# The last two pieces of every output product, multiplied by token tile instead of by piece

## The reference

```
x = layer_norm(ALPHA*x + 0.5*swiglu(x))          # 1024 -> 2816 -> 1024
y = concat(pool, gated conv, neighbourhood attention) @ w_out
x = layer_norm(ALPHA*x + y)
x = layer_norm(ALPHA*x + 0.5*swiglu(x))
```

```
x = x + 0.5*rms(swiglu(rms(x)))
x = x + rms(mixer(rms(x)))                       # MLA, GLA and RWKV branches, merged, @ w_out
x = x + rms(memory_attention(rms(x)))            # ... @ mem_wo
x = x + 0.5*rms(swiglu(rms(x)))
```

## Time and profile before

| | |
|---|---|
| median of three runs | 2997.88 us (2996.47 to 3000.35) |
| the profiled execution | 2998.23 us |
| its span, first to last instruction | 2996.4 us |
| TensorE, matmuls | 2800.4 us busy, 93% |
| VectorE | 1592.4 us, 53% |
| ScalarE | 1293.3 us, 43% |
| GpSimd | 477.8 us, 16% |
| mean granted TensorE clock | 0.965 |

### The profile page before, as it was taken

How to read it: one execution, slowest core, us unless ns; L and a number is a source line. 1 busy time by engine, 2 the same in 40 slices (tenths; PEclk the granted TensorE clock), 3 DMA queues, 4 the chain that set the end, 5 groups by cost and what they waited for, 6 DMA issues and landing times.

```text
span 2996.4 us, 51984 instructions
## 1 busy us (share of the span) xinstructions
PE 2800.4 (93%) x21700; PEld 2593.2 (87%) x21700; DVE 1592.4 (53%) x2184; ACT 1293.3 (43%) x1832; POOL 477.8 (16%) x199
## 2 busy tenths in 40 slices
PE   7999999999999999988889899999998878989998
PEld 7988899898889989987779788999988778888898
DVE  5566555656655565543545515555564274552555
ACT  3435443443543443444523454444444452344433
POOL 0000000000000000034423660000004451474000
PEclk9999999999999999998999999999999899999999
DMA  8755466675536646632322544665663331244563
GB/s 233 209 157 161 120 183 188 170 210 156 160 114 188 183 143 187 197 99 87 104 65 72 165 152 133 184 187 160 186 187 95 92 113 51 103 149 123 162 188 126
DMA packets 622827, 445.08 MB, mean 149 GB/s; under 512 B 27904, under 2 KB 589344, under 8 KB 622176
## 3 DMA queue, kind: packets, MB, share of 16 engines
q1 hardware_dynamic: 622688, 443.09, 49.8%
HBM read 441.99 MB, written 1.05 MB: 148 GB/s over the span
## 4 chain that ended last, share of the span: by engine, by line
PE 86%; DVE 9%; ACT 3%; issue 1%; DMA 0%; POOL 0%; SPq 0%; ACTq 0%; DVEq 0%; POOLq 0%
PE ps L373 19%; PE ps L374 18%; PE ps L375 18%; PE ps L389 7%; PE ps L390 7%; PE ps L391 7%; PE ps L630 1%; PE ps L606 1%; PE ps L1353 1%; ACT w_hi L645 1%; PE ps L1160 1%; PE ps L1061 1%; PE ps L1343 1%; DVE zT L1495 1%; DVE moments L908 1%
## 5 line engine op out<-in xcount | busy, mean ns | idle before, releaser
L373 PE MATMUL ps<-in_hi,w_hi 128*128 128x256 f32 x4352 | 1263.2, 290 | 69.5 <-POOL w_lo L814 31.1
L645 ACT ACTIVATE w_hi<-raw 128x1024 fp32r<-128x1024 f32 x800 | 844.9, 1057 | 947.1 <-PE ps L375 626.4
L374 PE MATMUL ps<-in_lo,w_hi 128*128 128x256 f32 x4352 | 1248.4, 287 | 0.0
L375 PE MATMUL ps<-in_hi,w_lo 128*128 128x256 f32 x4352 | 1247.6, 287 | 0.0
L814 DVE TENSOR_TENSOR w_lo<-raw,w_hi 128x1024 fp32r<-128x1024 f32 x606 | 742.7, 1226 | 742.8 <-ACT w_hi L645 741.7
L373 PEld LDWEIGHTS ps<-in_hi,w_hi 128*128 128x128 f32 x4352 | 852.9, 196 | 89.8 <-issue 32.4
L374 PEld LDWEIGHTS ps<-in_lo,w_hi 128*128 128x128 f32 x4352 | 852.9, 196 | 7.3 <-issue 0.5
L375 PEld LDWEIGHTS ps<-in_hi,w_lo 128*128 128x128 f32 x4352 | 851.9, 196 | 0.0
L814 POOL TENSOR_TENSOR w_lo<-raw,w_hi 128x1024 fp32r<-128x1024 f32 x194 | 477.2, 2468 | 2270.5 <-ACT w_hi L645 2269.7
L389 PE MATMUL ps<-w_hi,hid_hi 128*128 128x512 f32 x704 | 276.0, 392 | 0.0
L390 PE MATMUL ps<-w_lo,hid_hi 128*128 128x512 f32 x704 | 275.9, 392 | 0.0
(11 more groups left out here) (302 smaller groups left out, 2665.8 us busy)
## 6 DMA issues: line engine op xcount, KB each, us to landing
raw<-in_w_ffn_in SPq DMA_DIRECT2D x176, 512.0 KB, 3.8
raw<-in_w_mix SPq DMA_DIRECT2D x112, 512.0 KB, 3.8
raw<-in_ffn_w_gate SPq DMA_DIRECT2D x88, 512.0 KB, 4.1
raw<-in_ffn_w_up SPq DMA_DIRECT2D x88, 512.0 KB, 3.8
raw<-in_ffn_w_down SPq DMA_DIRECT2D x88, 512.0 KB, 3.6
raw<-in_w_ffn_out SPq DMA_DIRECT2D x88, 512.0 KB, 3.4
raw<-in_w_in SPq DMA_DIRECT2D x40, 512.0 KB, 3.8
raw<-in_w_out SPq DMA_DIRECT2D x32, 512.0 KB, 3.5
```

The lines of the kernel that those rows point to most:

```text
L373: nc.tensor.matmul(o, lh, rh, start=first, stop=False, **kw)
L374: nc.tensor.matmul(o, lh, rl, start=False, stop=False, **kw)
L375: return nc.tensor.matmul(o, ll, rh, start=False, stop=last, **kw)
L645: nc.scalar.activation(w_hi[:, e % SPLIT, :], raw[:, e % RAW, :], ACT.Copy).then_inc(sem("split_high"), 1)
```

## The change

The last two pieces of each output product are no longer multiplied one after the other. Both are multiplied into banks 0 and 1 (first 128 tokens) and then both into banks 2 and 3. The new function `last_two` writes the order out, and both `pe_rows` and `pe_ffn` end with it; for this the last round of the hardware loop in `pe_ffn` is taken out of the loop. `piece_used` of A is counted after A's matmuls on bank 3, in the second half, and that of B at the very end, as before. The wait for B's split and, in a SwiGLU, for the last hidden tile stands ahead of B's matmuls on bank 0.

```diff
--- before.py
+++ after.py
@@ -392,16 +392,33 @@
 
         def pe_rows(pe, e0, chunk):
 
-            for k in range(KD):
+            for k in range(KD - 2):
                 e = e0 + k
                 pe.wait_ge(sem("split_low"), e + 1)
                 pe.wait_ge(sem("in_ready"), chunk + k // 2 + 1)
                 for b in range(4):
-                    mm = three_rows(b, e, in_hi[:, k, :], in_lo[:, k, :], k == 0, k == KD - 1)
-                    if k == KD - 1 and b < 3:
-
-                        mm.then_inc(sem("rows_out"), 1)
+                    mm = three_rows(b, e, in_hi[:, k, :], in_lo[:, k, :], k == 0, False)
                 mm.then_inc(sem("piece_used"), 1)
+            pe.wait_ge(sem("in_ready"), chunk + KD // 2)
+
+            def ready(i):
+                pe.wait_ge(sem("split_low"), e0 + KD - 1 + i)
+
+            last_two(e0 + KD - 2, ready, [(in_hi[:, k, :], in_lo[:, k, :]) for k in (KD - 2, KD - 1)])
+
+        def last_two(e, ready, left):
+
+            for t in range(HALF):
+                for i in range(2):
+                    if t == 0:
+                        ready(i)
+                    for b in (2 * t, 2 * t + 1):
+                        mm = three_rows(b, e + i, *left[i], False, i == 1)
+                        if i == 1 and b < 3:
+
+                            mm.then_inc(sem("rows_out"), 1)
+                    if t == HALF - 1:
+                        mm.then_inc(sem("piece_used"), 1)
 
         WARM_BANK = 5
 
@@ -465,26 +482,31 @@
                                    k == 0, k == KD - 1)
                     mm.then_inc(sem("piece_used"), 1)
 
-            def down(j, it=0, last=False):
-                e = e0 + (FFN_PIECES - 1 if last else 3 * j + 4)
+            def hidden(j, e, it=0):
                 pe.wait_ge(sem("split_low"), e + 1 + it * RAW)
 
                 pe.wait_ge(sem("hidden_ready"), (ffn0 + n) * TILES + j + 1 + it * 2)
+
+            def down(j, it=0):
+                e = e0 + 3 * j + 4
+                hidden(j, e, it)
                 for b in range(4):
-                    mm = three_rows(b, e, hid_hi[:, j % 2, :], hid_lo[:, j % 2, :], j == 0, last)
-                    if last and b < 3:
-
-                        mm.then_inc(sem("rows_out"), 1)
+                    mm = three_rows(b, e, hid_hi[:, j % 2, :], hid_lo[:, j % 2, :], j == 0, False)
                 mm.then_inc(sem("piece_used"), 1)
 
             begin()
             gate_up(1)
             down(0)
-            with pe.Fori(0, TILES // 2 - 1) as it:
+            with pe.Fori(0, TILES // 2 - 2) as it:
                 for j in (2, 3):
                     gate_up(j, it)
                     down(j - 1, it)
-            down(TILES - 1, last=True)
+            gate_up(TILES - 2)
+            down(TILES - 3)
+            gate_up(TILES - 1)
+            e = e0 + FFN_PIECES - 2
+            last_two(e, lambda i: hidden(TILES - 2 + i, e + i), [(hid_hi[:, j % 2, :], hid_lo[:, j % 2, :])
+                                                                 for j in (TILES - 2, TILES - 1)])
 
         def pe_linear(pe, q0, e0, groups, chunk, together=1):
```

## The result

The changed kernel takes 3011.58 us (median of six runs, 3010.26 to 3012.01); the kernel before, run beside it, 2998.97 us (2996.47 to 3000.35). The ratio is 1.0042 with a 95% interval of 1.0029 to 1.0055: slower by 12.6 us. A second measurement of both gave 1.0030 (1.0019 to 1.0041), some 9 us. The forecast was 3022, and the range 3010 to 3031: the time lies in it, 10.4 us under the forecast and 1.6 us above the lower end.

What follows compares the result with a forecast made beforehand. TensorE is busy 93%; its tails end by a chain: A released, copy, subtraction, four banks. 13.6 + 4.8 - 1.3 + 2.4 + 4.5 = +24.0 us on 2998.23 gave 3022, range 3010 to 3031.

Steps and rivals of the forecast that it cites:

- Release of A, ten tails at 1.36: Six layer-norm and four second-block tails: A released two groups later delays copy, subtraction, norm and transposes; 13.6 us.
- The tail between the layers costs only the stall: Second block, between layers: fillers run up to the transposes, so A's later release costs nothing there.
- The stall, 8 x 0.6: Eight SwiGLU tails: TensorE waits for the last hidden tile before B's first group; 4.8 us.
- The last tail, -1.3 + 0.6: Kernel's end: banks 0 and 1 finished earlier gain 1.3 us; the stall of 0.6 is counted separately.
- B's split in time in the projections: Six products without a stall: B's split is ready when its group wants it; costed at nothing.
- The branch products, +2.4: Two branch-output products: GpSimd's moved subtraction delays the next chunk and the tail by 1.2 us each.
- The clock, +4.5: Longer TensorE idle before the transposes brings three half-clock falls more, 4.5 us; between none and 9 us.
- a fall costs 1.5 us: Price of one half-clock fall, from first transpose to first hidden matmul: 17.06 against 15.56 us.
- Faster: Rival: the norm starts on the early banks under TensorE's last groups; about -24 us, 2974; 4%.
- No change: Rival: A's later release is absorbed, leaving stalls and the last tail's gain; +3.5 us, 3001; 5%.
- Half of it: Rival: the 1.36 us holds, but the stall is under 0.3 and branch products gain; +12, 3010; 11%.
- The clock dominates: Rival: every exposed tail loses one more low stretch, 15 us in place of 4.5; +34.5, 3032; 12%.

Runs made afterwards that it cites:

- release_five: Changed kernel with group order A0 A1 A2 B0 A3 B1 B2 B3, A released after five groups; 1.0002 of the kernel before, +0.6 us.
- pure_delay: Kernel before, TensorE untouched; in ten tails VectorE subtracts or ScalarE copies twice for the piece replacing A; 1.0013 of before, +3.9 us.
- rows_only: Kernel before with the new order only in the six output projections (`pe_rows`); 1.0018 of before, +5.4 us.
- no_stall: Changed kernel with order A0 A1 A2 B0 B1 A3 B2 B3, three groups of A before B's first; 1.0023 of before, +6.9 us.
- ffn_only: Kernel before with the new order only in the eight SwiGLU products (`pe_ffn`); 1.0031 of before, +9.3 us.
- more_fillers: Changed kernel with five fillers more after each product, not between layers of the second block; 1.0040 of before.
- norm_first: Changed kernel, norm ahead of the split for A's successor on ScalarE and VectorE, GpSimd subtracting in the first block, fewer fillers; 2970.28 us, 0.9896 of before.
- norm_first_no_stall: norm_first with group order A0 A1 A2 B0 B1 A3 B2 B3; 2971.78 us beside 2966.83 for norm_first on the same chip.
- norm_first_old_order: Kernel before, its order A then B kept, with norm_first's rearrangement of ScalarE, VectorE, GpSimd and fillers; 2981.74 us, 0.9935 of before.

## Why the forecast was right, and where it was not

**Release of A, ten tails at 1.36: right.** The projections show it pure: +1.36 in each of four; release_five has half of it, and pure_delay lengthens the chain by 1.26 or 1.09 without a change on TensorE, and the tails with it. **The tail between the layers costs only the stall: right**, +0.69, and rows_only and no_stall have 14.97 and 15.01 there. **The stall, 8 x 0.6: right** to a tenth: the tail lengthens by 0.62 to 0.68, of which 0.58 is the gap on TensorE. The tails that have both show 2.05 to 2.07 where 1.96 was forecast. **The last tail, -1.3 + 0.6: right**, -0.62. These terms sum to 17.1 in the forecast and 17.9 in the traces.

**B's split in time in the projections: right.** TensorE's groups by line for the changed kernel (busy us, mean ns of one, idle before and what ended it): the first matmul of a group, first in the SwiGLUs, then in the projections:

```profile
L389 PE MATMUL ps<-w_hi,hid_hi 128*128 128x512 f32 x704 | 276.8, 393 | 3.4 <-DVE hid_lo L896 3.4
...
L389 PE MATMUL ps<-w_hi,in_hi 128*128 128x512 f32 x192 | 75.3, 392 | 8.8 <-DVE in_lo L868 7.8 <-ACT arena L811 0.9
```

The first idles 8 x 0.42 = 3.4 us, all for hid_lo; the second never for a piece's w_lo.

**The branch products, +2.4: the size and the sign were wrong.** The first in_lo is short and the next chunk's products end late, as told, but the second chunk is 0.75 late, not 1.2: in_lo gained 1.35, the two products lost 2.97 - 0.87 = 2.10. And between the branch product's A and the memory product's A the time is 0.6 shorter: 0.75 later by the chunk, and 3.4 us less at the lower clock, which at 0.41 each are 1.4 (an estimate from the rows above, not shown by a run). So -0.6 and -0.5 instead of twice +1.2. The forecast put a delay of a chunk down as a delay of the stage; what the stage lasts also depends on where in it the clock falls. The Trainium skill, "SBUF — State Buffer", section "SBUF: two separate sides", says that of VectorE and GpSimd whoever starts first blocks the other for a whole instruction. These rows agree with it within 0.3 us. An in_lo of 0.68 alone came when a GpSimd subtraction of 2.4 us, begun at 1708.74, had some 0.6 us to go, and took 1.06, where the rule would give some 1.25 (an estimate, 0.57 + 0.68); two products of 0.87 alone took 2.97 with one subtraction beside them, where it would give some 3.3 (2.40 + 0.87).

**The clock, +4.5: wrong in sign, and the main miss.** The forecast took three falls more, each at 1.5 us, the difference of the two rows of one tail. By count it was near: the changed kernel has 218 and 225 us at half clock in its two traces, the kernel before 210 and 208. The price was wrong. The traces have the same stretch, from the first transpose after the memory product to the first hidden-tile matmul, in both layers of every kernel:

| kernel | idle before the transposes | clock falls on | stretch |
|---|---|---|---|
| before (two traces), ffn_only | 1.05 | gate matmuls (5 of 6) | 17.05 |
| | 1.05 | nothing (1 of 6) | 15.56 |
| more_fillers | 0.25 | nothing (2 of 2) | 15.56 |
| release_five | 1.72 | nothing (2 of 2) | 15.56 |
| pure_delay | 2.14 | nothing (2 of 2) | 15.55 |
| norm_first (two traces), norm_first_no_stall | 0.81, 1.42 | nothing (6 of 6) | 15.55 |
| norm_first_old_order | 2.10 | last transposes and gate matmuls, twice as long (2 of 2) | 17.55 |
| after (two traces), rows_only, no_stall | 2.40 | transposes (8 of 8) | 15.85 |

TensorE in the changed kernel, windows (0.58 is nearly the lower level, 1.00 the upper) and the timeline after the first layer's memory product; they answer to the earlier trace rows.

```profile
1843.00:1847.00 4.00, 3.18 (x15) 0.58 0.00 0
1848.00:1852.00 4.00, 3.95 (x33) 1.00 0.00 0
```

```profile
1843.82 3.54 PE L440 MATMUL ps<-const,zT 128*128 128x128 f32 x16 [2.40 <-DVE zT L1046]
...
1848.05 0.39 PE L373 MATMUL ps<-in_hi,w_hi 128*128 128x256 f32 x1 [0.70 <-DVE in_lo L880]
...
1859.66 0.40 PE L389 MATMUL ps<-w_hi,hid_hi 128*128 128x512 f32 x1
```

With the longer idle the clock is down earlier: on the transposes, which are short and followed by a wait for VectorE's chunks anyway (1.34 us before, 0.70 now). There a fall costs 0.29 us, not 1.5, and where the kernel before had its fall on the gate matmuls the change gains 1.2 (17.05 to 15.85). The forecast's step "a fall costs 1.5 us" took the price of one place for the price of all. Nor does the length of the idle tell whether a fall comes: 2.10 us and 2.14 us before the same transposes came with a long one in norm_first_old_order and with none in pure_delay. The two tails of the earlier trace rows could not bear it out either, since both had an idle of 1.05. What decides it stays open.

Over the whole kernel the stretches that this moves sum to -4.4 us, where single ones differ by 1.5 to 4.4 us between two traces of the kernel before. In the memory tails the change gains 1.7 of it. Which part of the rest is owed to the change and which to chance stays open.

The Trainium skill, "TensorE: Matmul & The Clock Gate", section "What's actually happening", says that activity releases the throttle, so longer idling should bring more time at half clock. The changed kernel's traces agree (218 and 225 us against 210 and 208); pure_delay's does not, with 211 us at twice the idle. No run shows that this time has one price.

**The range held with some luck.** In sum the forecast had 17.1 for the tails, 2.4 for the branches and 4.5 for the clock, and the traces have 17.9, -1.2 and, for all that lies between the tails, -4.4. The tails carry the result. The other two terms were both too high, and what stands in the clock's place is below the least that the forecast gave the clock (0 us), so that 12.6 lies under the lowest sum, +13; the range begins at 3010, 1.6 us below the measured time.

**The rivals.** "Faster" was ruled out by the queues' order, and norm_first shows that it was indeed that: with the norm ahead the same TensorE order gains. The rival's -24 us came out at 145.9 - 172.2 = -26 in the tails, of which the order of the pieces is 11. "No change" is refuted by the tails: nothing of the 1.36 us is absorbed in any of the ten. "Half of it", 3010, came closest in time, but for another reason: its stall under 0.3 is refuted by no_stall, and of its gain at the branches, 2.6, there is 1.2. "The clock dominates" wanted 15 us for longer idling: pure_delay has ten tails with the idle of the changed kernel less 0.1 to 0.3 us, and costs 3.9 in all.

## What to carry to other kernels

Before finishing a result earlier, ask in which order its consumer's queue stands: here banks finished 1.36 us sooner were worth 11 us with the norm ahead of the next stage's split, and cost 12 behind it (the stall of the last hidden tile included), because the same reordering held a ring buffer longer and that release stood first in the queue. A wait that is moved costs what stands behind it on the chain, and nothing if that is something else (no_stall against norm_first_no_stall). Price a clock fall by what runs during it, not by one example, and trace a kernel twice before reading a difference of a few microseconds in one stretch as an effect.

## What the hardware showed that was not expected

Two traces of one unchanged kernel agree within 0.04 us in every tail and differ by up to 4.4 us in a stretch of 108 us between two tails, by where TensorE is granted 1.2 GHz. In two long stretches 10 us more at that level went with 4.2 and 4.4 us of time; one fall cost 1.5 us on gate matmuls and 0.29 on transposes that are followed by a wait. The idle ahead of such a fall did not tell whether it came: with 1.05 us it came in five of six, with 1.72 and 2.14 in none of four, with 2.10 in two of two, with 2.40 in eight of eight. Raising the idle by 1.26 and 1.09 us at ten places, 11.9 us in all, cost 3.9 us of time (1.2 to 6.6). And at the branches' end a shift of GpSimd's subtraction by 1.4 us turned VectorE's 2.42 and 0.87 us into 1.06 and 2.97: the wait for a neighbour moved from one operation to another.
